# Streamed operands of five matmul stages read in pieces, alternating between the two halves of the tokens

## The chip, the cores and the metric

The kernel runs on one core of one Trainium2 chip. The metric is the device time of one execution in microseconds; lower is better. Two runs of the kernel before gave 889.39 and 889.61 us, a median of 889.5 us.

## The reference, cut to what matters

Two transformer-like blocks are applied in turn to x of shape (1, 256, 1024) in float32: 256 tokens, model width 1024. Nearly all the arithmetic is in dense projections:

```python
xn = rms_norm(h, norm1_g)                       # first block
proj = xn @ w_in                                # 1024 -> 5136
for n, y in enumerate((y_a, y_b, y_c, y_d)):    # four branches, width 512
    merged += sigmoid(xn @ w_gate[n] + b_gate[n]) * (y @ w_branch[n])
h = h + merged @ w_out
h = h + square(relu(rms_norm(h) @ w_ff1)) @ w_ff2          # 1024 -> 4096 -> 1024
h = h + sigmoid(rms_norm(h) @ w_ple_gate + b) * (p @ w_ple)
...                                             # second block, on the result
x = x + g1 * (merged_2 @ w_out_2)
x = x + g2 * ((silu(hh @ w_gate_2) * (hh @ w_up_2)) @ w_down_2)   # 1024 -> 2816 -> 1024
return rms_norm(x, normf_g)
```

Beside the projections there are small parts (spatial gating, gated linear attention, banded attention, a convolution, an mLSTM and a second attention), and a vector of modulations computed from `ada_w_2`.

## The kernel before, in words

Activations are kept transposed, features on the 128 partitions and the 256 tokens along the free dimension (`T = 256`). To keep float32 accuracy with the reduced float32r type of the matrix engine, every operand is split into a high part, rounded to float32r, and a low part, the remainder. Each product is then made of three matmuls: high weights by low tokens (L1054), low weights by high tokens (L1056), high by high (L1057).

Weights arrive from HBM in 298 slabs of 8 units (a unit is a 128x128 block of a weight matrix; `SLAB = 8`), 512 KB each, in the order that `plan()` and `NAMES` give. `sync_program` issues the loads into `raw` (5 buffers), ScalarE's `high_part` (L1991, its instruction is L2002) writes `whi`, and VectorE's `low_part` (L1091, its instruction is L1103) writes `wlo`. Both have 4 buffers (`NHL = 4`), so the two engines can be up to four slabs ahead, and both wait for the matmuls of the slab four before.

`tensor_program` walks over `NAMES`. For a stage of kind "F", which is nearly all of them, the weights are the stationary operand (a weight load of 128 columns ahead of each matmul) and the 256 tokens of one feature block are streamed against them. A PSUM bank of 512 values takes two output blocks of 256 tokens, `half(0)` and `half(1)`; for each pair the loop runs over the K input blocks, and in each over the two output blocks. `bank()` takes three PSUM banks by turns and waits until the pair three before has been drained by ScalarE or VectorE. In stages of kind "T" it is the other way round: the activations are stationary and the weights are streamed, 512 (once 272) columns per matmul (L1025 to L1027). Four stages are `WIDE` and stream 258 tokens.

Between products the queue of TensorE also holds the small parts, as steps at fixed slab numbers (`STEPS`, called through `tick()`). Among these are matmuls in plain float32: transposes of `aacc` (L753), a broadcast in the mLSTM (L790), and single small products that `plain()` issues (L601). VectorE's queue has its own steps at fixed slab numbers; the products with `ada` (L1435) lie between slabs 66 and 149.

The stages that the change touches are "F" stages that aren't `WIDE`: `gt0` to `gt3` (the gates, 64 units each) and `br0` to `br3` (the branches, 32 units each), which run by turns from 131 to 274 us; `ff1` (256 units, 296 to 386 us); `ff2` (256 units, 386 to 476 us, it streams `Fhi` and `Flo`); and `dn` (132 units, 820 to 865 us, it streams `Uhi` and `Ulo`). Three matmuls per unit make 768 for the gates, 384 for the branches, 768 for ff1, 768 for ff2 and 396 for dn: 3084 of the 7171 matmuls that the program states. The stages between and after them, `wo` (from 274 to 296 us), `ple`, `pg`, all `zg` and `zu` (711 to 820 us for those that aren't wide), `dy` and `dz`, are not touched.

In the compiled program's layout every streamed activation block of 256 values (1024 bytes per partition) begins 64 bytes past a multiple of 512 bytes, and every 128-column weight block (512 bytes per partition) begins 128 bytes past one. Two unused tensors, `gap0` and `gap3`, are part of that layout.

Of the kernel before, what the change touches and what calls it, by code (L numbers as in the profile page):

```python
# [179 lines left out]
ROPE = (0, 2, 1, 3)  # L180

LATE = 214

BETWEEN = {40: 3, 68: 7, 183: 5}
STEPS = {
# [87 lines left out]
def build(nc, A, out):  # L273
# [16 lines left out]
    with ctx:  # L290
# [158 lines left out]
        half = lambda j: slice(j * T, (j + 1) * T)  # L449
# [53 lines left out]
        def low(s):  # L503
            return lo_v.at(s)
# [90 lines left out]
        def tensor_program(pe):  # L595
# [3 lines left out]
            def plain(b):  # L599

                pe.matmul(banks[b][:, 0:128], ones[:, :], mats[:, 0:128], start=True, stop=True)  # L601
# [6 lines left out]
            def total(tag, b):  # L608
                w.wait_ge(*ones_v.at("set"))
                w.wait_ge(*added.at(tag, 3))  # L610
                pe.matmul(banks[b][:, 0:T], ones[:, :], acc, start=True, stop=True).then_inc(*summed.up(tag))
# [340 lines left out]
            def bank(name, p):  # L952
                if (name, p) in ASIDE:
                    return banks[ASIDE[name, p]]
                if len(held) >= 3:
                    w.wait_ge(*drained(*held[-3]))
                held.append((name, p))
                return banks[(len(held) - 1) % 3]

            def weights(n=1):  # L960
                nonlocal u
                s, o = u // SLAB, u % SLAB
                if o == 0:
                    w.wait_ge(*hi.at(s))
                    w.wait_ge(*low(s))
                u += n
                at = slice(o * 128, (o + n) * 128)
                return whi[:, s % NHL, at], wlo[:, s % NHL, at]

            def tick():  # L970
                for task in pe_steps.get(u / SLAB - 1, ()):
                    if task in tasks:
                        next(tasks[task], None)
# [34 lines left out]
            for name in NAMES[1:]:  # L1008
                kind, _, _, _, m, K = PLAN[name]
                if name == "ga":  # L1010
                    u += SLAB
                    tick()
                    continue
                if kind == "T":
                    bs = [bank(name, tt) for tt in range(2)]
                    for k in range(K):
                        xh, xl = ready(name, k)
                        wh, wl = weights(PLAN[name][4] // 128)
                        if name == "gk":
                            w.wait_ge(*hi.at(8))  # L1020
                            w.wait_ge(*low(8))
                            wh, wl, m = Ghi[:, k, :], Glo[:, k, :], T + 16
                        for tt in range(2):
                            o, ts, last = bs[tt][:, 0:m], slice(tt * 128, (tt + 1) * 128), k == K - 1
                            pe.matmul(o, xl[:, ts], wh, start=k == 0, stop=False)  # L1025
                            pe.matmul(o, xh[:, ts], wl, start=False, stop=False)  # L1026
                            i = pe.matmul(o, xh[:, ts], wh, start=False, stop=last)  # L1027
                            of = [(name, tt)] * last + [("slab", u // SLAB - 1)] * (tt == 1 and u % SLAB == 0)
                            if (name, tt, last) == ("gv", 1, True):
                                of.append(("slab", u // SLAB))  # L1030
                            if of:
                                i.then_inc(*mm.up(*of))
                        if u % SLAB == 0:
                            tick()
                    continue
                wide = name in WIDE
                for p in range(-(-m // 2)):
                    nt = min(2, m - 2 * p)
                    b = bank(name, p)
                    if wide:  # L1040
                        second = SECOND[name, p]
                        os = [b[:, 0:T + 2], banks[second][:, 0:T + 2]]
                        w.wait_ge(*(red_v.at(5) if name == "mq0" else root.at("r3") if name == "mq1"
                                    else ml_s.at("root", 1, 1)))
                        if name == "zu0":
                            w.wait_ge(*att2_s.at("p", 3, 0))
                    else:
                        os = [b[:, half(j)] for j in range(2)]
                    for k in range(K):
                        xh, xl = ready(name, k)  # L1050
                        for j in range(nt):
                            wh, wl = weights()
                            last = k == K - 1 and j == nt - 1
                            pe.matmul(os[j], wh, xl, start=k == 0 and (wide or j == 0), stop=False,  # L1054
                                      skip_group_check=not wide)
                            pe.matmul(os[j], wl, xh, start=False, stop=False, skip_group_check=not wide)  # L1056
                            i = pe.matmul(os[j], wh, xh, start=False, stop=k == K - 1 if wide else last,  # L1057
                                          skip_group_check=not wide)
                            of = [(name, p)] * last + [("slab", u // SLAB - 1)] * (u % SLAB == 0)
                            if of:  # L1060
                                i.then_inc(*mm.up(*of))
                            if u % (SLAB // 2) == 0 and not last:
                                tick()
                    if (name, p) == ("mq0", 0):
                        w.wait_ge(*aw_v.at(3))
                        w.wait_ge(*aw_v.at("sum"))
                        pe.matmul(banks[6][:, 0:T], ones[:, :], aw2[:, 0:T], start=True, stop=True
                                  ).then_inc(*aw_pe.up("aw"))
                        plain(7)
                    tick()  # L1070
                if name == "ple":
                    total("r3", 3)
                if name == "dz":
                    w.wait_ge(*added.at("r5", 6))
                    for h in range(2):
                        pe.matmul(banks[3 + h][:, 0:1], acc[:, TOK[h]], ones[:, 0:1], start=True, stop=False)
                    for h in range(2):
                        w.wait_ge(*sq.at("r5", 7, h))
                        pe.matmul(banks[3 + h][:, 0:1], t512[1][:, T + 128 * h:T + 128 * h + 128], ones[:, 0:1],
                                  start=False, stop=True).then_inc(*summed.up("r5", h))  # L1080
                    for h in range(2):
                        w.wait_ge(*rstd.at("r5", h))
                        pe.matmul(banks[5 + h][:, 0:128], ones[:, :], t512[0][:, TOK[h]], start=True, stop=True
                                  ).then_inc(*spread_pe.up(h))

        def vector_program(v):
# [4 lines left out]
            def low_part(s):  # L1091
                if s >= NS or s in lows:
                    return
                lows.add(s)
                w.wait_ge(*hi.at(s))
                if s >= NHL:
                    w.wait_ge(*mm.at("slab", s - NHL))
                if s in (8, 9, 10):
                    x, y = narrow(s, raw[:, s % NRAW, :], Ghi)
                    v.tensor_tensor(narrow(s, raw[:, s % NRAW, :], Glo)[1], x, y.bitcast(F32), ALU.subtract  # L1100
                                    ).then_inc(*lo_v.up(s))
                    return
                v.tensor_tensor(wlo[:, s % NHL, :], raw[:, s % NRAW, :], whi[:, s % NHL, :].bitcast(F32),  # L1103
                                ALU.subtract).then_inc(*lo_v.up(s))
# [865 lines left out]
            for name in NAMES:  # L1970
                for what, n in EVENTS[name]:
                    if what == "pair":
# [3 lines left out]
                        continue  # L1976
                    if n == int(n) and n >= 1 and n != LATE:
                        low_part(int(n) + 3)
                    for task in v_steps.get(n, ()):
                        if task in tasks:  # L1980
                            next(tasks[task], None)
                    if n == LATE:
                        low_part(int(n) + 3)
# [534 lines left out]
        def gpsimd_program(g):  # L2518
# [13 lines left out]
            g.memset(mpad[:, :, 0:3], 0.0).then_inc(*mpad_g.up("set"))  # L2532

        programs = ((sync_program, nc.sync), (tensor_program, nc.tensor), (vector_program, nc.vector),
                    (scalar_program, nc.scalar), (gpsimd_program, nc.gpsimd))
        for program, _ in programs:
# [127 lines left out]
```

## Time and profile before

| | |
|---|---|
| runs | 889.39 and 889.61 us, median 889.5 us |
| profiled execution, span | 888.8 us, from the first to the last instruction |
| around the span | 0.7 us between the span and the median of the runs |
| TensorE busy | 878.6 us (99%) |
| VectorE busy | 729.9 us (82%) |
| ScalarE busy | 569.2 us (64%) |
| DMA | 189.83 MB, mean 214 GB/s |
| granted TensorE clock | 0.996 of full speed, mean over the span |

No time of the profiled execution other than its span is recorded, so the span plus 0.7 us stands for it. In the profile a matmul's start is recorded and its end is modelled; matmuls overlap, so a row's duration (276 ns) isn't what a matmul costs. What it costs is the distance between the starts of two that follow each other, called the pitch below. "PEld" is the loading of the stationary operand, which runs beside the matmul before.

### The profile page before, as it was taken

The numbers are of one execution on the slowest core, as the hardware profiler recorded it, in microseconds if no ns is written. First come the engines' busy times: TensorE is split into PE (matmuls) and PEld (weight loads), VectorE is DVE, ScalarE is ACT, GpSimd is POOL, SyncE is SP. The second block draws the span as 40 slices with busy tenths as digits, with TensorE's granted clock in tenths as the row PEclk, the third lists the DMA queues.
The fourth block names the chain that finished last, engine by engine and source line by source line (L and its number), as shares of the span: only waits on it lengthen the run. The fifth ranks groups of instructions, "written<-read, shape, count | busy, mean of one in ns | idle before, by whom it ended". The sixth has DMA issues, their size and how long they took to land.

```text
span 888.8 us, 18455 instructions
## 1 busy us (share of the span) xinstructions
PE 878.6 (99%) x7342; PEld 855.4 (96%) x7342; DVE 729.9 (82%) x1168; ACT 569.2 (64%) x838; POOL 1.9 (0%) x9
## 2 busy tenths in 40 slices
PE   8999999999999999999999999999999999999997
PEld 7999989999999999999999999899999999999996
DVE  6788999899999999898966999988788885555544
ACT  7858467675686777654446868677785664444542
POOL 0000000000000000000000000000000000000000
PEclk9999999999999999999999999999999999999998
DMA  8856446556875789988855576654545566566541
GB/s 313 284 194 224 157 150 207 166 173 229 277 274 189 272 289 347 355 318 324 317 189 170 175 218 197 197 164 127 171 146 173 192 196 195 195 193 197 186 158 48
DMA packets 54550, 189.83 MB, mean 214 GB/s; under 512 B 6193, under 2 KB 8641, under 8 KB 54337
## 3 DMA queue, kind: packets, MB, share of 16 engines
q1 hardware_dynamic: 54320, 188.65, 63.4%
q8 instruction: 59, 0.97, 0.4%
q14 instruction: 27, 0.21, 0.1%
q10 hardware_dynamic: 144, 0.00, 0.0%
HBM read 186.53 MB, written 1.05 MB: 211 GB/s over the span
## 4 chain that ended last, share of the span: by engine, by line
PE 96%; DVE 1%; ACT 1%; DMA 1%; issue 0%; SPq 0%; DVEq 0%; ACTq 0%
PE bank L1054 28%; PE bank L1056 28%; PE bank L1057 28%; PE bank L1025 2%; PE bank L1027 2%; PE bank L1026 2%; DMA H<-in_xT 1%; PE bank L753 1%; PE bank L989 0%; PE bank L996 0%; PE bank L992 0%; ACT whi L2002 0%; DVE wlo L1103 0%; PE bank L855 0%; PE bank L728 0%
## 5 line engine op out<-in xcount | busy, mean ns | idle before, releaser
L2002 ACT ACTIVATE whi<-raw 128x1024 fp32r<-128x1024 f32 x294 | 308.4, 1057 | 191.5 <-PE bank L1057 183.9
L1103 DVE TENSOR_TENSOR wlo<-raw,whi 128x1024 fp32r<-128x1024 f32 x294 | 356.5, 1220 | 86.6 <-ACT whi L2002 85.9
L1054 PE MATMUL bank<-Alo,whi 128*128 128x256 f32 x1336 | 373.5, 280 | 0.0
L1057 PE MATMUL bank<-Ahi,whi 128*128 128x256 f32 x1336 | 369.4, 277 | 0.0
L1056 PE MATMUL bank<-Ahi,wlo 128*128 128x256 f32 x1336 | 369.4, 277 | 0.0
L1054 PEld LDWEIGHTS bank<-Alo,whi 128*128 128x128 f32 x1336 | 250.9, 188 | 2.8 <-issue 2.6
L1056 PEld LDWEIGHTS bank<-Ahi,wlo 128*128 128x128 f32 x1336 | 251.0, 188 | 0.4 <-issue 0.2
L1057 PEld LDWEIGHTS bank<-Ahi,whi 128*128 128x128 f32 x1336 | 250.9, 188 | 0.0
L1056 PE MATMUL bank<-Fhi,wlo 128*128 128x256 f32 (+1 forms) x320 | 88.8, 278 | 0.0
L1057 PE MATMUL bank<-Fhi,whi 128*128 128x256 f32 (+1 forms) x320 | 88.8, 278 | 0.0
L1054 PE MATMUL bank<-Flo,whi 128*128 128x256 f32 x256 | 70.9, 277 | 0.0
L1056 PEld LDWEIGHTS bank<-Fhi,wlo 128*128 128x128 f32 x320 | 60.3, 188 | 0.0
L1057 PEld LDWEIGHTS bank<-Fhi,whi 128*128 128x128 f32 x320 | 60.3, 188 | 0.0
L1435 DVE SCALAR_TENSOR_TENSOR aacc<-araw,shb,aacc 128x1024 f32<-128x1024 f32 x42 | 53.7, 1279 | 1.3 <-DMA araw<-in_ada 1.3
L1054 PE MATMUL bank<-Ylo,whi 128*128 128x256 f32 x192 | 53.6, 279 | 0.0
L1056 PE MATMUL bank<-Yhi,wlo 128*128 128x256 f32 x192 | 53.0, 276 | 0.0
L1057 PE MATMUL bank<-Yhi,whi 128*128 128x256 f32 x192 | 53.0, 276 | 0.0
L1202 DVE SCALAR_TENSOR_TENSOR cv<-ypad,cols,cv 128x256 f32<-128x256 f32 x120 | 51.3, 477 | 0.1
L1057 PE MATMUL bank<-Uhi,whi 128*128 128x256 f32 x176 | 48.6, 276 | 0.0
L1054 PE MATMUL bank<-Ulo,whi 128*128 128x256 f32 x176 | 48.6, 276 | 0.0
L1056 PE MATMUL bank<-Uhi,wlo 128*128 128x256 f32 x176 | 48.6, 276 | 0.0
L1054 PEld LDWEIGHTS bank<-Flo,whi 128*128 128x128 f32 x256 | 48.1, 188 | 0.0
(432 smaller groups left out, 1380.8 us busy)
## 6 DMA issues: line engine op xcount, KB each, us to landing
raw<-in_stream SPq DMA_DIRECT2D x298, 512.0 KB, 4.3
araw<-in_ada SPq DMA_DIRECT2D x48, 512.0 KB, 5.9
TB<-in_TB SPq DMA_DIRECT2D x1, 1536.0 KB, 6.9
a8r<-a SPq DMA_DIRECT2D x16, 64.0 KB, 3.9
out<-H SPq DMA_DIRECT2D x4, 256.0 KB, 2.9
bc<-in_bc SPq DMA_DIRECT2D x1, 896.0 KB, 6.0
H<-in_xT SPq DMA_DIRECT2D x1, 512.0 KB, 7.6
mats<-in_mats SPq DMA_DIRECT2D x1, 449.0 KB, 7.1
```

The costliest lines, as they stand in the source:

```text
L753: i = pe.transpose(banks[6 + j // 4][:, j % 4 * 128:j % 4 * 128 + 128], aacc[cb % 2][:, j * 128:j * 128 + 128], ident)
L1025: pe.matmul(o, xl[:, ts], wh, start=k == 0, stop=False)
L1026: pe.matmul(o, xh[:, ts], wl, start=False, stop=False)
L1027: i = pe.matmul(o, xh[:, ts], wh, start=False, stop=last)
L1054: pe.matmul(os[j], wh, xl, start=k == 0 and (wide or j == 0), stop=False, skip_group_check=not wide)
L1056: pe.matmul(os[j], wl, xh, start=False, stop=False, skip_group_check=not wide)
L1057: i = pe.matmul(os[j], wh, xh, start=False, stop=k == K - 1 if wide else last, skip_group_check=not wide)
L1103: v.tensor_tensor(wlo[:, s % NHL, :], raw[:, s % NRAW, :], whi[:, s % NHL, :].bitcast(F32), ALU.subtract).then_inc(*lo_v.up(s))
L1202: v.scalar_tensor_tensor(out=o, in0=y, scalar=c, in1=o, op0=ALU.mult, op1=ALU.add).then_inc(*conv_v.up("tap", j, ct))
L1435: v.scalar_tensor_tensor(out=o, in0=araw[:, n % 3, :], scalar=csil[:, k:k + 1], in1=o, op0=ALU.mult, op1=ALU.add).then_inc(*ada_v.up(n))
L2002: a.activation(whi[:, s % NHL, :], raw[:, s % NRAW, :], ACT.Copy).then_inc(*hi.up(s))
```

## The change

A table gives a piece length to each of the five stages. The 256 streamed tokens are taken as two halves of 128; the stream takes the first piece of the first half, the first piece of the second half, the second piece of the first half, and so on. The output in PSUM is addressed with the same pattern, so that every result lands where it did before. With the piece length e there are 256/e pieces per matmul, each e values (4e bytes) long. Two pieces that follow each other lie 512 bytes apart, less or more one piece. Nothing else changes: the number and order of instructions, the weight loads, the waits and the transfers stay.

```diff
+PIECES = {"gt": 8, "br": 4, "ff1": 16, "ff2": 32, "dn": 64}
...
+            def in_pieces(name, x):
+
+                e = PIECES.get(name if name in PIECES else name[:2])
+                return x if e is None else x.rearrange("p (h c e) -> p c h e", h=2, e=e)
+
...
                     else:
-                        os = [b[:, half(j)] for j in range(2)]
+                        os = [in_pieces(name, b[:, half(j)]) for j in range(2)]
                     for k in range(K):
-                        xh, xl = ready(name, k)
+                        xh, xl = (in_pieces(name, x) for x in ready(name, k))
```

## Rows read from the trace of the kernel before

**Rows 1.** The page: busy time by engine; the chain that ended last, by engine.
```profile
PE 878.6 (99%) x7342; PEld 855.4 (96%) x7342; DVE 729.9 (82%) x1168; ACT 569.2 (64%) x838; POOL 1.9 (0%) x9
...
PE 96%; DVE 1%; ACT 1%; DMA 1%; issue 0%; SPq 0%; DVEq 0%; ACTq 0%
```

**Rows 2.** Waits: who waited for whom, us in total, times, longest us.
```profile
ACT whi L2002 <- PE bank L1057: 183.9, 132, 3.6
DVE wlo L1103 <- ACT whi L2002: 85.9, 82, 2.7
...
PE bank L989 <- ACT whi L2495: 1.7, 2, 0.9
```

**Rows 3.** Stretches: length, busy us (x instructions) of PE, PEld, DVE, ACT, POOL, clock, DMA.
```profile
191.00:263.00 72.00, 72.00 (x633) 70.71 (x632) 70.92 (x110) 51.02 (x78) 0.00 (x0) 1.00 0.73 250
296.00:386.00 90.00, 90.00 (x795) 89.92 (x794) 85.52 (x103) 66.76 (x93) 0.00 (x0) 1.00 0.92 332
386.00:476.00 90.00, 90.00 (x797) 90.00 (x795) 70.76 (x83) 40.03 (x45) 0.00 (x0) 1.00 0.77 274
722.00:820.00 98.00, 98.00 (x868) 98.00 (x867) 56.89 (x56) 47.38 (x54) 0.00 (x0) 1.00 0.63 201
820.00:865.00 45.00, 45.00 (x400) 45.00 (x399) 23.75 (x25) 22.68 (x26) 0.00 (x0) 1.00 0.55 181
```

**Rows 4.** Timeline of PE in dn and in wo2: start us, duration us, instruction.
```profile
839.83 0.28 PE L1056 MATMUL bank<-Uhi,wlo 128*128 128x256 f32 x1
...
840.96 0.28 PE L1057 MATMUL bank<-Uhi,whi 128*128 128x256 f32 x1
...
679.84 0.28 PE L1054 MATMUL bank<-Mlo,whi 128*128 128x256 f32 x1
...
680.90 0.28 PE L1054 MATMUL bank<-Mlo,whi 128*128 128x256 f32 x1
```

**Rows 5.** Line L1057: duration ns min/median/max, first and last start.
```profile
L1057 PEld LDWEIGHTS bank<-Uhi,whi x176: 187/188/188, 820.1 to 879.6; 128*128 128x128 f32 x176
...
L1057 PEld LDWEIGHTS bank<-Mhi,whi x64: 192/192/192, 676.4 to 698.7; 128*128 128x128 f32 x64
```

**Rows 6.** Timeline of PE after a break at 711 us.
```profile
711.40 0.28 PE L1057 MATMUL bank<-Ahi,whi 128*128 128x256 f32 x1
...
711.76 0.28 PE L1057 MATMUL bank<-Ahi,whi 128*128 128x256 f32 x1
...
711.99 0.28 PE L1056 MATMUL bank<-Ahi,wlo 128*128 128x256 f32 x1
...
712.33 0.28 PE L1056 MATMUL bank<-Ahi,wlo 128*128 128x256 f32 x1
```

**Rows 7.** Timeline of PE: plain float32 matmuls of 256 and of 128 columns.
```profile
565.57 1.02 PE L790 MATMUL bank<-diag,ones 128*128 128x256 f32 x4
...
444.89 1.04 PE L753 MATMUL bank<-mats,aacc 128*128 128x128 f32 x8
```

**Rows 8.** The lines L790 and L753: duration ns min/median/max.
```profile
L790 PE MATMUL bank<-diag,ones x8: 378/379/379, 565.6 to 608.6; 128*128 128x256 f32 x8
...
L753 PE MATMUL bank<-mats,aacc x48: 272/273/328, 259.2 to 445.7; 128*128 128x128 f32 x48
```

**Rows 9.** Timeline of PEld after a break at 510.8 us.
```profile
510.82 0.19 PEld L1054 LDWEIGHTS bank<-Fhi,whi 128*128 128x128 f32 x1 [0.41 <-issue]
510.93 0.19 PEld L1056 LDWEIGHTS bank<-Fhi,wlo 128*128 128x128 f32 x1
```

**Rows 10.** Timeline of PE: float32r matmuls of 512 columns.
```profile
569.89 0.39 PE L1025 MATMUL bank<-whi,Alo 128*128 128x512 f32 x1
...
570.80 0.39 PE L1026 MATMUL bank<-wlo,Ahi 128*128 128x512 f32 x1
```

## The prediction

> **What bounds the kernel now.** I read the page first, for the busy shares and the chain of waits: TensorE is busy for 99% of the span and holds 96% of the chain that ended last [rows 1]. The view of the waits says the same from the other side: ScalarE, which makes the high weights, waits 183.9 us for the matmuls of earlier slabs, VectorE waits 85.9 us behind ScalarE, and the longest entry of TensorE itself is 1.7 us [rows 2]. So the weights are there in time and the time is the number of matmuls times their pitch. The number doesn't change; only the pitch can move.
>
> The pitch comes from the stretches. In the pure product stretch from 820 to 865 us, which is the stage dn, 400 matmuls touch 45.00 us; some three of them only overlap the start, so 397 fill it: 113.4 ns each [rows 3]. The timeline gives the same: ten pitches in 840.96 - 839.83 = 1.13 us, 113 ns [rows 4]. The stretch 722 to 820 has 865 in 98.00 us, again 113.3 ns, though VectorE is busy 58% of it and DMA moves 201 GB/s; the stretch 386 to 476 has it too (794 in 90.00, among them a few smaller ones) at 79% and 274 GB/s [rows 3]. So the pitch doesn't depend on what the other engines and the transfers do to the memory. The granted clock in all these rows is 1.00, the upper level of 2.4 GHz, at which 256 columns are 106.7 ns. Of the 113.3 ns, 6.6 ns aren't columns.
>
> Are they a fixed cost? Three views say no. First, the same instruction with the same operand positions has another pitch elsewhere: in wo2 nine pitches take 680.90 - 679.84 = 1.06 us, 117.8 ns [rows 4], and there the weight loads of L1057 take 192 ns where those of dn take 188 ns [rows 5]. Second, after a break at 711 us three pitches take 711.76 - 711.40 = 0.36 us, and soon after three take 712.33 - 711.99 = 0.34 us, 120 ns and then 113 ns without any change of instruction [rows 6]. Third, plain float32 matmuls, which stream at half the rate, show almost nothing on top of their columns: the four of L790 last 1.02 us together and 0.379 us each, so three pitches are 0.64 us, 214 ns, against 213.3 ns for 2 x 256 columns (the rounding of the row leaves +/- 3 ns); the eight of L753 give (1.04 - 0.273)/7 = 109.6 ns against 106.7 ns for 2 x 128 [rows 7, 8]. 512 columns of float32r take (570.80 - 569.89)/4 = 228 ns against 213.3 ns [rows 10]. What remains over the columns is 1 to 3 ns for a stream at half rate and 6.6, 11 or 14 ns at full rate, in steps of some 4.5 ns (117.8 - 113.3; 192 - 188). I read such a step as one meeting: the stream of tokens and the stream of the next weights read the same partitions at once, and where they come to the same part of the memory one of them stalls.
>
> **The change part by part.** Instructions, their order, waits and transfers stay, so nothing is queued anew behind a waiting instruction. What moves is the order of addresses in 3084 matmuls.
>
> Before: in one pitch the weight stream covers 512 bytes and the token stream 1024. If memory parts repeat every 512 bytes, the token stream overtakes the weights exactly once per matmul wherever the two start. That is the one step that the 113.3 ns hold. A float32 stream at half rate never overtakes. After: the halves lie 512 bytes apart, so both look alike to the rule, and by turns the token stream goes twice over each piece while the weights go once over the same length. Its mean speed is that of the weights; it only swings ahead and back by half a piece, 2e bytes: 8 bytes for br, 16 for gt, 32 for ff1, 64 for ff2, 128 for dn. The starts are 64 bytes apart (64 and 128 past the multiple of 512). Pieces of 4, 8 and 16 then never meet the weights, 32 just reaches, 64 goes past.
>
> The price of the step for a stage: floor 109.2 ns (the 109.6 ns of L753, whose rounding allows 109; 109.2 is 106.7 plus the 2.5 ns that the half-rate rows leave), so 113.3 - 109.2 = 4.1 ns are to be had. The weight loads allow it: the first two after the break at 510.8 us start 0.11 us apart while no matmul holds them [rows 9], which bounds a load's own pitch to 105 to 115 ns. That row is the weak place; if 113 were the loads' own pitch, nothing would be gained (rival B).
>
> - gt, br, ff1, ff2: 768 + 384 + 768 + 768 = 2688 matmuls by 4.1 ns = 11.0 us. Bounds: 0 below; above, 6.6 ns each (the columns alone) = 17.7 us.
> - dn: 396 matmuls. With pieces of 64 the stream still passes the weights. One meeting as before would give 0, none -1.6 us, two +1.6 us. I take 0.
> - The jumps themselves: no row shows a stream or a PSUM write with a jump in it. I take 0, since the nearest rows, all contiguous, show a cost only with meetings. Bounds: nothing, to one step (4.1 ns) for each jump; 256/e - 1 jumps are 31, 63, 15, 7 and 3 per matmul, 66,084 in all, 271 us. A range that wide is carried by rivals D and E.
> - Cover by VectorE: from 191 to 263 us it is busy 70.92 of 72.00 us [rows 3]. Some 576 changed matmuls lie there, so TensorE alone would need 72.0 - 2.4 = 69.6 us, and VectorE becomes late by up to 1.3 us. It can hand most of that on, since it may be four slabs ahead and the stretch after it is looser; ff1 needs 85.52 us of VectorE and would have 90.0 - 3.1 = 86.9 [rows 3], so it holds. I take 0.5 us lost, bounds 0 and 2.
> - After effects: wo, ple, pg, dy and dz start from another relation of the two streams and may fall into the 117.8 ns rhythm of wo2. All of wo at it costs 192 x 4.5 ns = 0.9 us. I take 0.3, bounds 0 and 2.
>
> Sum against the profiled execution: 888.8 + 0.7 - 11.0 + 0.5 + 0.3 = 879.3 us. The span plus 0.7 us is the median of the runs, so the forecast for the runs is 879.3 us too, 1.1% less.
>
> What the trace can't answer is the price of jumps in the output. The Trainium skill's page "PSUM — Partial Sum Buffer", section "Specifications (TRN2)", gives cachelines of 8 bytes and says "any non-contiguous AP slows matmuls significantly"; no run here shows it, since every output of the kernel before is contiguous. By its letter this is rival E; all pieces here hold at least two whole pairs, so by the reason it gives, the changed stages would lose little.
>
> **The rivals.** B, nothing changes: the 113 ns are the pitch of the weight loads or a fixed cost. For it: it is the commonest pitch by far and very even. Against it: rows 4 to 6. It gives 889.5 us, give or take 1.
>
> C, slower by meetings where pieces are long. Place: ff2 and dn. With pieces of 32 and 64 the stream swings past the weights 256/2/e times, 4 and 2 times per matmul, where it passed once before. Price: 3 x 4.1 ns x 768 + 1 x 4.1 x 396 = 9.4 + 1.6 = 11.0 us, against 1920 x 4.1 ns = 7.9 us gained in the other three stages: 889.5 - 7.9 + 11.0 = 892.6 us. It decides from the point where the real distance of the two streams is under 64 bytes; the 64 bytes are those of the start addresses, and when the reads of each begin relative to the other I can't see. With a distance under 32 bytes ff1 turns too (8 meetings, +22 us).
>
> D, each jump costs: an address pattern of three dimensions that loses one cycle of the lower clock level, 0.83 ns (a fifth of the step), at each of 66,084 jumps would add 55 us: 944 us, with gates and branches hit most (+26 and +52 ns per matmul). A third of that still is 908 us. For it: no row shows such a pattern running free. Against it: nothing.
>
> E, writing in pieces halves the pace: 214 ns, the float32 pitch of [rows 7], for 113: 3084 x 0.10 = 310 us, 1200 us.
>
> **How the numbers follow.** The forecast has 0.45, with its own range 876 to 884 us. B 0.17, C 0.21 (885 to 899), D 0.14, E 0.03. The measurement of this kernel can tell about 2% from no change, which is 17.8 us. Faster by more needs 5.8 ns of the 6.6 per matmul gone, or a slower pitch elsewhere cured as well: 0.03, out of the forecast's tail. Slower by more than 2% is most of D, E and the bad end of C: 0.14. Within: 0.83. The range is 875.5 to 903 us: it leaves 0.04 below and about 0.15 above. The likeliest case, C and B together lie within it.
>
> **What would show it.** In the profile after: pitch of 109 ns in gt, br, ff1 and ff2 (the stretch of ff2 holds 825 matmuls in 90 us where it held 794), 113 in dn and in the untouched zg and zu, weight loads at 188 ns throughout, waits of ScalarE for TensorE smaller. C would show as ff2 slower and gt faster; D as a pitch that rises with the number of jumps, br worst; B as 113 everywhere. Wrong would be the idea itself if the pitch falls evenly in all five stages whatever the piece, dn included, or if it rises most where pieces are short.

## The result and the profile after

The changed kernel takes 911.17 us (910.23 and 912.11) against 889.5: the two medians make 1.0244, and the ratio with its interval is 1.0252 (95% interval 1.0236 to 1.0269). It is slower by 21.7 us where 10.2 us less was forecast, and outside the range. Two executions in the runs below had a much lower granted clock (1476.88 us at 0.56 in the kernel before, 1096.78 us at 0.75 in e9) and are left out of every median and ratio. The profiled execution has a span of 910.8 us, 22.0 more than before.

TensorE is as busy as it was, it only does the same number of matmuls at a longer pitch, and ScalarE waits longer for it. First the page and the waits of the kernel after:

```profile
PE 901.1 (99%) x7342; PEld 877.7 (96%) x7342; DVE 732.1 (80%) x1168; ACT 572.7 (63%) x838; POOL 1.9 (0%) x9
...
ACT whi L2009 <- PE bank L1064: 195.7, 136, 3.6
```

PE's busy time rose by 22.5 us, VectorE's by 2.2: the cover by VectorE that the prediction worried about was never used up, because nothing got faster. Now the stretches of the kernel after (length, busy us and instructions of PE, PEld, DVE, ACT, POOL, clock, DMA share and rate): ff1, ff2, pg and dn.

```profile
308.00:402.00 94.00, 94.00 (x786) 93.94 (x785) 85.05 (x102) 67.69 (x92) 0.00 (x0) 1.00 0.90 317
404.00:497.00 93.00, 93.00 (x787) 93.00 (x786) 70.55 (x82) 39.64 (x44) 0.00 (x0) 1.00 0.76 262
503.00:526.00 23.00, 23.00 (x196) 22.95 (x195) 19.34 (x30) 19.07 (x33) 0.00 (x0) 1.00 0.57 181
842.00:887.00 45.00, 45.00 (x400) 45.00 (x399) 23.92 (x26) 22.39 (x26) 0.00 (x0) 1.00 0.58 184
```

ff1 has 786 matmuls in 94 us, so 94.00/783 = 120 ns each, where it had 90.00/792 = 114 [rows 3]. ff2 has 93.00/784 = 119 ns for 90.00/794 = 113. dn has 400 in 45 us, exactly what it had. The timelines of PE give each stage's pitch without the small matmuls in between (start us, duration us). First gates (16 pitches apart), then a branch, ff1 and ff2 (24 pitches apart each):

```profile
139.97 0.28 PE L1061 MATMUL bank<-Alo,whi 128*128 128x256 f32 x1
...
141.94 0.28 PE L1063 MATMUL bank<-Ahi,wlo 128*128 128x256 f32 x1
...
280.50 0.30 PE L1064 MATMUL bank<-Yhi,whi 128*128 128x256 f32 x1
...
283.54 0.29 PE L1064 MATMUL bank<-Yhi,whi 128*128 128x256 f32 x1
...
330.52 0.28 PE L1061 MATMUL bank<-Alo,whi 128*128 128x256 f32 x1
...
333.40 0.28 PE L1061 MATMUL bank<-Alo,whi 128*128 128x256 f32 x1
...
440.52 0.28 PE L1063 MATMUL bank<-Fhi,wlo 128*128 128x256 f32 x1
...
443.37 0.28 PE L1063 MATMUL bank<-Fhi,wlo 128*128 128x256 f32 x1
```

That is 1.97/16 = 123 ns in the gates (pieces of 8), 3.04/24 = 126.7 in the branches (4), 2.88/24 = 120.0 in ff1 (16) and 2.85/24 = 118.8 in ff2 (32), against 113.3 in all of them before. [rows 3] and [rows 4] show that for ff2 and dn; here are gates and a branch of the kernel before, 24 pitches apart, 2.72 us each:

```profile
142.75 0.28 PE L1056 MATMUL bank<-Ahi,wlo 128*128 128x256 f32 x1
...
145.47 0.28 PE L1056 MATMUL bank<-Ahi,wlo 128*128 128x256 f32 x1
...
267.74 0.28 PE L1057 MATMUL bank<-Yhi,whi 128*128 128x256 f32 x1
...
270.46 0.28 PE L1057 MATMUL bank<-Yhi,whi 128*128 128x256 f32 x1
```

By pitches the loss is 768 x 10.0 + 384 x 13.4 + 768 x 6.7 + 768 x 5.5 ns = 7.7 + 5.1 + 5.1 + 4.2 = 22.1 us. By the starts in the traces it is a little less: gt0 starts at 130.59 us before and 130.63 after, ple, the first stage behind ff2, at 475.92 and 497.45. So gates and branches took 12.3 us more, ff1 5.0 and ff2 4.1, 21.5 in all; ple and pg, which aren't changed, added 1.0 to 1.1, and some 0.5 us came back behind them. Together that is the 22.0 us of the spans. The first matmul of ple, before and after:

```profile
475.92 0.28 PE L1054 MATMUL bank<-Blo,whi 128*128 128x256 f32 x1
```

```profile
497.45 0.28 PE L1061 MATMUL bank<-Blo,whi 128*128 128x256 f32 x1
```

dn, with pieces of 64, gives nothing. The shorter the piece the longer the pitch, but not in proportion to the jumps: 7, 15, 31 and 63 jumps cost 5.5, 6.7, 10 and 13.4 ns.

### The profile page after: what moved, and what is told of

The parts are those of the page before. It is cut to its first block, busy times and chain, and to the rows that moved or that the text cites. A ratio compares the mean times of both kernels' runs of the same rounds, so it can differ in the third digit from the quotient of the medians.

```text
span 910.8 us, 18455 instructions
## 1 busy us (share of the span) xinstructions
PE 901.1 (99%) x7342; PEld 877.7 (96%) x7342; DVE 732.1 (80%) x1168; ACT 572.7 (63%) x838; POOL 1.9 (0%) x9
## 4 chain that ended last, share of the span: by engine, by line
PE 91%; ACT 4%; DVE 3%; issue 1%; DMA 1%; SPq 0%; DVEq 0%; ACTq 0%
PE bank L1061 27%; PE bank L1063 27%; PE bank L1064 27%; ACT whi L2009 1%; PE bank L1034 1%; PE bank L1032 1%; PE bank L1033 1%; DMA H<-in_xT 1%; PE bank L755 1%; DVE wlo L1110 1%; PE bank L996 0%; PE bank L1003 0%; PE bank L999 0%; DVE mqk L1538 0%; PE bank L857 0%
## 5 line engine op out<-in xcount | busy, mean ns | idle before, releaser
L1061 PE MATMUL bank<-Alo,whi 128*128 128x256 f32 x1336 | 378.0, 283 | 0.0
L1064 PE MATMUL bank<-Ahi,whi 128*128 128x256 f32 x1336 | 373.8, 280 | 0.0
L1063 PE MATMUL bank<-Ahi,wlo 128*128 128x256 f32 x1336 | 373.8, 280 | 0.0
L1061 PE MATMUL bank<-Ylo,whi 128*128 128x256 f32 x192 | 55.5, 289 | 0.0
L1064 PE MATMUL bank<-Yhi,whi 128*128 128x256 f32 x192 | 55.0, 286 | 0.0
L1063 PE MATMUL bank<-Yhi,wlo 128*128 128x256 f32 x192 | 54.9, 286 | 0.0
```

## The experiments

Most of them use one device: the stages zg2 to zu10 of the kernel before are 18 equal stretches of 48 matmuls with no other matmul in between, all at 113.3 ns [rows 3]. A table gives each its own address pattern, so that one execution measures 18 patterns. Its core, on the kernel before:

```diff
+def pieces(e, d=128, off=0):
+    return off, [[e, 128 // e], [d, 2], [1, e]]
+def onward(e, hop):
+    return 0, [[2 * e, 128 // e], [e + hop, 2], [1, e]]
+def shift(off):
+    return off, [[1, 256]]
...
-                        os = [b[:, half(j)] for j in range(2)]
+                        os = [in_slot(name, "w", b[:, half(j)]) for j in range(2)]
...
+                            xh, xl = (in_slot(name, "r", x) for x in (xh, xl))
...
+                            wh, wl = wh[:, cols_of], wl[:, cols_of]
```

`in_slot` replaces the free dimensions by those of the table, `cols_of` cuts the weight columns. A pitch in the tables below is a mean over 24 pitches in the later part of the stage, from the starts in the timeline. Where single pitches swing (with pieces of 4 they go from 120 to 134 ns), another choice of 24 moves the mean by up to 0.5 ns.

**e1: reading or writing, and the size.**

> The kernel before, with patterns only in the quiet stages zg2 to zu10 (48 matmuls each, one pattern per stage): read and written in pieces of 64, 32, 16, 8, 4 (zg2 to zg4); read only in those sizes, written in one run (zg5 to zg7); written only (zg8 to zg10); zu4, zu7, zu10 as before. In the read-only and write-only stages the tokens land in another place in PSUM, so those products stand for other tokens. Theory R (the order of reads costs): the read-only stages have the pitches of the read-and-write ones, as in the changed kernel 113, 119, 120, 123 and 127 ns, and the write-only ones stay at 113. Theory W (the jumps in PSUM cost): the other way round. Both: they share it.

| pieces of | 64 | 32 | 16 | 8 | 4 |
|---|---|---|---|---|---|
| read and written | 113.3 | 118.8 | 120.0 | 123.3 | 126.8 |
| read only | 113.3 | 118.8 | 120.0 | 123.3 | 126.8 |
| written only | 113.3 | 113.3 | 113.3 | 113.3 | 113.3 |

Timeline of PE of e1, 24 pitches apart: zg7, read in pieces of 4, and zg10, written in pieces of 4:

```profile
780.05 0.29 PE L1107 MATMUL bank<-Ahi,wlo 128*128 128x256 f32 x1
...
783.09 0.30 PE L1107 MATMUL bank<-Ahi,wlo 128*128 128x256 f32 x1
...
813.27 0.28 PE L1107 MATMUL bank<-Ahi,wlo 128*128 128x256 f32 x1
...
815.99 0.28 PE L1107 MATMUL bank<-Ahi,wlo 128*128 128x256 f32 x1
```

3.04 us against 2.72 us. The five pitches of the changed kernel come back in another stage, on other data, so they belong to the pattern and not to gates or ff2. All of it is in the reads. Theory R holds, theory W falls.

**e8 and e9: the same at full size.** The reads alone and the writes alone of the change, each in all five stages:

```diff
-                        os = [in_pieces(name, b[:, half(j)]) for j in range(2)]
+                        os = [b[:, half(j)] for j in range(2)]
```

> The changed kernel with the reads in pieces and the writes in one run, in all five stages with the sizes of the change; the tokens of those stages land in another place in PSUM, so their results stand for other tokens. Theory R: the whole loss of the change stays, 911 us. Theory W: 889.5 us.

911.32 us, ratio to the kernel before 1.025 (1.0233 to 1.0266): the whole loss.

```diff
-                        xh, xl = (in_pieces(name, x) for x in ready(name, k))
+                        xh, xl = ready(name, k)
```

> The changed kernel with the writes in pieces and the reads in one run, in all five stages with the sizes of the change; again the results stand for other tokens. Theory R: 889.5 us within 1 us. Theory W, or the rule that output which isn't contiguous slows a matmul: 911 us or most of the way there.

889.37 us, ratio 1.0002 (0.9992 to 1.0012). A stretch of e8, then one of e9, each 94 us in ff1 and what follows it:

```profile
308.00:402.00 94.00, 94.00 (x786) 93.94 (x785) 85.07 (x102) 67.66 (x92) 0.00 (x0) 1.00 0.89 317
```

```profile
308.00:402.00 94.00, 94.00 (x831) 93.96 (x831) 88.96 (x100) 64.95 (x88) 0.00 (x0) 1.00 0.92 329
```

786 matmuls, as in the changed kernel, against 831. With 128 weight columns, writing PSUM in pieces of 4 to 64 values costs nothing that can be measured here. The sentence of the Trainium skill's page "PSUM — Partial Sum Buffer", section "Specifications (TRN2)", that was rival E's ground doesn't hold for these patterns.

**e7: pieces of 64 everywhere.**

```diff
-PIECES = {"gt": 8, "br": 4, "ff1": 16, "ff2": 32, "dn": 64}
+PIECES = {"gt": 64, "br": 64, "ff1": 64, "ff2": 64, "dn": 64}
```

> The changed kernel with pieces of 64 in all five stages; it computes what the kernel before does. Theory P (order within 256 bytes, which pieces of 64 leave as it was): all five stages at 113.3 ns and the time of the kernel before, within 1 us. Theory J with a cost per jump: 3 jumps per matmul would show as under 1 us per 0.3 ns of pitch.

889.41 us, ratio 1.0003 (0.9993 to 1.0012): as said, with 113.3 ns in gates, branches, ff1 and ff2. (Run beside e7 to e9, the kernel before gave 12 times from 887.9 to 888.5 us and 5 from 889.5 to 889.9; what may part them follows.) But its profiled execution took 894.9 us, and there dn was not at 113. Timeline of PE of e7, in zg4 (24 pitches apart), a stage that this kernel doesn't touch:

```profile
744.46 0.28 PE L1063 MATMUL bank<-Ahi,wlo 128*128 128x256 f32 x1
...
747.29 0.28 PE L1063 MATMUL bank<-Ahi,wlo 128*128 128x256 f32 x1
```

2.83/24 = 117.9 ns, and so from zu1 to dz, 1440 matmuls, 6 us; while pa and wo2, at 117.8 in the kernel before, ran at 113.3. It began inside zg1, right after a single pitch of 135 ns. So the rhythm of [rows 4] at 680 us is not tied to the stage or the pattern: it is a second steady relation that an execution may fall into after a disturbance and then keeps. e9's profiled execution (887.71 us) shows wo2 in the quicker rhythm too, 205 matmuls in the stretch that held 197 in the kernel before (shown under e11):

```profile
676.00:699.00 23.00, 23.00 (x205) 23.00 (x204) 19.89 (x33) 14.01 (x22) 0.00 (x0) 1.00 0.55 178
```

The 288 matmuls of pa and wo2 at 4.5 ns are 1.3 us, about what lies between the two groups of times of the kernel before. That this is what parts them is likely, but only profiled executions show their stages. So a difference of 1 us between two medians of these kernels says little.

**e3 and e6: is it the weight stream?** Both cut the weight columns, from 128 to 64 or 32.

> The kernel before, with fewer weight columns in zg2 to zg10, so that the weight stream is shorter; the other output rows of those stages aren't computed anew. 64 columns with the tokens in one run, then in pieces of 64, 32, 16, 8, 4 (read and written), zu5 to zg8 the same with 32 columns (one run, 32, 16, 8, 4), then 64 columns with pieces of 8 and 4 read only and written only. Theory R as meetings: with 64 columns the extra time falls to about half, with 32 to a quarter, so 109 to 111 ns in one run and under 113 in most pieces. Theory J or W: a length of the weight stream changes nothing, 120 ns and more for pieces of 16 and below. A pitch set by the weight loads themselves would fall to 109 ns or below in every stage.

| pieces of (read and written) | one run | 64 | 32 | 16 | 8 | 4 |
|---|---|---|---|---|---|---|
| 64 weight columns | 113.3 | 113.3 | 120.0 | 120.5 | 123.3 | 129.2 |
| 32 weight columns | 113.3 | | 118.3 | 120.0 | 123.3 | 126.8 |

Timeline of PE of e3, 24 pitches apart, with 32 weight columns: zu5 in one run, zu7 in pieces of 4:

```profile
761.34 0.28 PE L1105 MATMUL bank<-Alo,whi 128*32 128x256 f32 x1
...
764.06 0.28 PE L1105 MATMUL bank<-Alo,whi 128*32 128x256 f32 x1
...
784.22 0.29 PE L1105 MATMUL bank<-Alo,whi 128*32 128x256 f32 x1
...
787.26 0.29 PE L1105 MATMUL bank<-Alo,whi 128*32 128x256 f32 x1
```

2.72 us and 3.04 us, to the last digit what they are with 128 columns. A weight stream a quarter as long changes neither the 6.6 ns over the columns nor the cost of pieces. The theory of the prediction falls here on both counts, and so does a pitch set by the weight loads. Two things don't fit. With 64 columns pieces of 32 and of 4 cost 1 to 3 ns more than with 128 or with 32. And 64 columns with pieces of 8 or of 4 written only, which read in one run, ran at 119.0, where in e1 and e9, with 128 columns, such writes cost nothing. Both stages followed stages read in pieces, so something carried over from those may be it, and so may the writes together with 64 columns; this wasn't tried apart.

> The kernel before, with 32 weight columns in single quiet stages (the other output rows aren't computed anew) and the start of the tokens, of the weights or of both shifted, all read in one run; those products stand for other data. Tokens shifted by 16, 32, 48, 64 values; weights shifted by 16, 32, 48, 64, 96; both by 16, both by 32; at the end tokens alone by 16 and 64 with all 128 weight columns. Theory M (the two streams meet, and the place of the weights counts): shifting the weights moves the pitch as shifting the tokens does, and shifting both alike brings back 113.3 ns. Theory T (only the place of the tokens counts): shifting the weights leaves 113.3 ns, shifting the tokens gives 120, 118, 118.5 and 113 or 118 as with 128 columns, and shifting both gives the pitch of the tokens' shift.

With 32 weight columns every one of the eleven patterns ran at 113.3 ns, tokens or weights or both shifted. With 128 columns tokens shifted by 16 gave 120.0, by 64 113.3. Timeline of PE of e6, 24 pitches apart, tokens shifted by 16 values: zg2 with 32 weight columns, zg9 with 128:

```profile
722.45 0.28 PE L1110 MATMUL bank<-Ahi,wlo 128*32 128x256 f32 x1
...
725.17 0.28 PE L1110 MATMUL bank<-Ahi,wlo 128*32 128x256 f32 x1
...
798.94 0.28 PE L1110 MATMUL bank<-Ahi,wlo 128*128 128x256 f32 x1
...
801.82 0.28 PE L1110 MATMUL bank<-Ahi,wlo 128*128 128x256 f32 x1
```

So with a long weight stream the place of the tokens does cost (2.72 us against 2.88). I read that as the two streams meeting, though shifted weights weren't tried with 128 columns. But it is a cost on top of the 113.3 ns that the layout of the kernel before already avoids, not the one inside them. Neither theory as stated passes: M said that the place of the weights would show at 32 columns, T that the tokens' would.

**e2: shifts with all the weight columns.**

> The kernel before, with the start of the streamed tokens in zg2 to zu10 shifted by 8, 16, 32, 48, 64, 80, 96, 112, 120 values against the weights: in zg the read is in one run, in zu in pieces of 16, both written in one run. The products there stand for shifted tokens. Theory R as meetings of the two streams: the pitch depends on the shift, a run in one between 109 and 118 ns, and in pieces of 16 there are shifts at 109 ns (never meeting) beside shifts above 120 ns. Theory J (a jump costs by itself, wherever the weights are): no dependence on the shift by more than the alignment, 113 in one run and about 120 in pieces. Theory W: all 113.

| shift of the tokens (values) | 8 | 16 | 32 | 48 | 64 | 80 | 96 | 112 | 120 |
|---|---|---|---|---|---|---|---|---|---|
| in one run | 118.3 | 120.0 | 117.8 | 118.5 | 117.8 | 120.0 | 117.8 | 118.5 | 117.3 |
| pieces of 16 | 120.0 | 120.0 | 120.0 | 120.0 | 120.0 | 120.0 | 120.0 | 120.0 | 120.0 |

In one run, shifts that differ by 64 values (16 and 80, 48 and 112, 32 and 96) agree, and 16 and 48 don't: the repeat is 64 values, 256 bytes, not the 512 that the prediction took. No shift comes near 109 ns. 64 gave 117.8 here and 113.3 in e6, the two rhythms of one pattern. The single pitches of 32 and 96 run as those of 64 do (117, 118 and 118 ns by turns), so their 117.8 may be that rhythm and not the shift. In pieces of 16 the place of the weights doesn't matter at all.

**e4: other distances between the two regions.**

> The kernel before, with other distances between the two regions read by turns (read only, written in one run, always from the first four feature blocks, so those products stand for other data): pieces of 16 at distances of 128, 32, 136, 144, 160, 192, 224, 256 and 64 values, pieces of 4 at 128, 144, 160, 192, 256, 512 and 64. Theory R as meetings with a repeat of 512 bytes: 128, 256 and 512 alike, 192 and 64 (half a repeat off) different. Theory J: all distances alike, about 120 ns for 16 and 127 for 4. Theory W: all 113.

| distance (values) | 128 | 32 | 64 | 136 | 144 | 160 | 192 | 224 | 256 | 512 |
|---|---|---|---|---|---|---|---|---|---|---|
| pieces of 16 | 120.0 | 123.3 | 120.0 | 120.0 | 120.0 | 123.3 | 120.0 | 123.3 | 120.0 | |
| pieces of 4 | 126.6 | | 126.5 | | 123.3 | 120.0 | 126.6 | | 126.3 | 126.5 |

Distances that are whole multiples of 64 values are alike, those with half of 64 over (32, 160, 224) differ. That gives the repeat of 256 bytes a second time, now from one operand alone, and theory J, by which every distance is alike, falls.

**e5: jumps that keep the order.**

> The kernel before, with other read patterns in single quiet stages (read only, written in one run, from the first four feature blocks; those products stand for other data). First onward patterns, in which every second piece is taken from a place farther on so that the address within 256 bytes runs on as in one run: pieces of 4 with a hop of 64 and 128 values, of 8, 16 and 32 with a hop of 64. Then the same with hops that break it: pieces of 4 with 32, 16, 8, pieces of 16 with 32 and 16. Then pieces of 64 by turns at distances of 160 and 192, of 32 at 64, of 2 at 128. Theory P (what counts is the order of addresses within 256 bytes): the whole onward patterns stay at 113 ns (or 118, its second rhythm) however many jumps they have, the broken ones and pieces of 64 at 160 lie above, pieces of 64 at 192 stay at 113. Theory J (each jump costs): onward pieces of 4 cost as much as pieces of 4 by turns, 127 ns, and pieces of 2 more, over 130.

| pattern, read only | jumps | pitch |
|---|---|---|
| onward, pieces of 4, hop 64 or 128 | 63 | 113.3 |
| onward, pieces of 8, 16, 32, hop 64 | 31, 15, 7 | 113.3 |
| onward, pieces of 4, hop 16 | 63 | 113.3 |
| onward, pieces of 4, hop 32 or 8 | 63 | 120.0 |
| onward, pieces of 16, hop 32 or 16 | 15 | 117.8 |
| by turns, pieces of 64, distance 192 | 3 | 113.3 |
| by turns, pieces of 64, distance 160 | 3 | 120.0 |
| by turns, pieces of 32, distance 64 | 7 | 118.7 |
| by turns, pieces of 2, distance 128 | 127 | 166.7 |

Timeline of PE of e5, 24 pitches apart: zg2 (onward, pieces of 4, hop 64), zg9 (pieces of 64 at 160), zu9 (pieces of 64 at 192), zu10 (pieces of 2):

```profile
721.49 0.28 PE L1108 MATMUL bank<-Alo,whi 128*128 128x256 f32 x1
...
724.21 0.28 PE L1108 MATMUL bank<-Alo,whi 128*128 128x256 f32 x1
...
798.44 0.28 PE L1108 MATMUL bank<-Alo,whi 128*128 128x256 f32 x1
...
801.32 0.28 PE L1108 MATMUL bank<-Alo,whi 128*128 128x256 f32 x1
...
804.41 0.28 PE L1111 MATMUL bank<-Ahi,whi 128*128 128x256 f32 x1
...
807.13 0.28 PE L1111 MATMUL bank<-Ahi,whi 128*128 128x256 f32 x1
...
815.83 0.34 PE L1110 MATMUL bank<-Ahi,wlo 128*128 128x256 f32 x1
...
819.83 0.34 PE L1110 MATMUL bank<-Ahi,wlo 128*128 128x256 f32 x1
```

This is the pair that decides. 63 jumps that leave the order of addresses within 256 bytes as it was take 2.72 us for 24, the same as none; 3 jumps that break it by 32 values take 2.88. A jump by itself is free; the order within 256 bytes is what is paid for. Pieces of 64 are one whole repeat each, so by turns between halves 512 bytes apart they are, to the memory, the order of before: that is why dn didn't move. (Pieces of 4 with a hop of 16 are free too, which theory P as stated doesn't say: not every other order costs.)

**e10: what the 6.6 ns are, and which costs are the token stream's own.**

> The kernel before, with 32 weight columns in single quiet stages, where e3 and e6 left 113.3 ns (other output rows aren't computed anew, and the products stand for other or fewer tokens). Streams of 64, 128, 192 and 240 values in one run; the same 8 and the same 64 values read over and over; then onward pieces of 4 with hops of 32 and 8, of 16 with 32 and 16, pieces of 64 at a distance of 160, pieces of 2, pieces of 4 at 160; at the end 8 values over and over with 128 weight columns. If the 6.6 ns over the columns are a fixed cost of a matmul: pitches of 33, 60, 87 and 107 ns for the four lengths (n/2.4 + 6.6), unless a load holds them at some floor. If they are lost along the stream: n x 0.4427, so 28, 57, 85 and 106 ns. If only addresses matter, 8 values over and over change the pitch, to 107 or far above 113; if it is a fixed cost, it stays 113.3. For the broken patterns: if their cost came from the weight stream, 32 columns bring them to 113.3; if from the token stream alone, they keep 120, 120, 118, 118, 120, 167, 120.

| stream of (32 weight columns, one run) | 128 | 192 | 240 | 256 (e3) | 8 values, 32 times over |
|---|---|---|---|---|---|
| pitch | 60.0 | 86.7 | 106.7 | 113.3 | 110.0 |
| less n/2.4 | 6.7 | 6.7 | 6.7 | 6.7 | 3.3 |

Timeline of PE of e10: zg3, 128 values, and zg5, the same 8 values over and over, 24 pitches apart:

```profile
728.55 0.22 PE L1116 MATMUL bank<-Alo,whi 128*32 128x128 f32 x1
...
729.99 0.22 PE L1116 MATMUL bank<-Alo,whi 128*32 128x128 f32 x1
...
746.64 0.27 PE L1118 MATMUL bank<-Ahi,wlo 128*32 128x256 f32 x1
...
749.28 0.27 PE L1118 MATMUL bank<-Ahi,wlo 128*32 128x256 f32 x1
```

1.44/24 = 60.0 ns for 128 columns of 53.3. The time over the columns is 6.7 ns at all four lengths: up to 256 columns it is a cost per float32r matmul and not one along the stream. Half of it goes when the addresses never leave 32 bytes, so it isn't wholly fixed, but that stream computes nothing of use (the same 64 values over and over stay at 113.3). Beyond 256 columns it is more: the 258 columns of mq1 in the kernel before take 2.90/24 = 120.8 ns, 13.3 over, and 512 columns 228, 14 over [rows 10]. Whether a longer stream pays twice wasn't tried, nor were other lengths with 128 weight columns.

```profile
518.90 0.28 PE L1054 MATMUL bank<-Fhi,whi 128*128 128x258 f32 x1
...
521.80 0.28 PE L1054 MATMUL bank<-Fhi,whi 128*128 128x258 f32 x1
```

(64 values gave pitches of 28 to 38 ns and decide nothing.) The broken patterns at 32 weight columns: onward pieces of 4 with hops of 32 and 8 fell from 120.0 to 113.3, so their cost in e5 hung on the weight stream; onward pieces of 16 with hops of 32 and 16 stayed at 117.8, pieces of 64 at 160 at 120.0, pieces of 2 at 166.7, pieces of 4 at 160 at 120.0. 8 values over and over took 111.7 ns with 128 weight columns.

**e11: breaking the second rhythm.** Two small float32 products more in the kernel before.

```diff
-BETWEEN = {40: 3, 68: 7, 183: 5}
+BETWEEN = {40: 3, 68: 7, 183: 5, 219: 3, 223: 3}
```

> The kernel before (same results), with one small plain float32 product more at the start of pa and one at the start of wo2, stages that run at 117.8 ns with weight loads of 192 ns. If the slower rhythm is a lasting relation between the token stream and the weight loads, and the break at 711 us ended it by its float32 product, these two put 288 matmuls to 113.3 ns: -1.3 us, +0.4 us for the products, so about 888.6 for 889.5. If the rhythm belongs to the place in the program, nothing changes but +0.4 us.

889.34 us, ratio 1.0002 (0.9993 to 1.0011): no change that these times can show; the 0.9 us less that was the first expectation is as large as the spread between executions. In its trace wo2 did go to 113.3 ns, 205 matmuls in a stretch that held 197, while pa stayed at 117.8. The stretch 676 to 699 us, of the kernel before and then of e11:

```profile
676.00:699.00 23.00, 23.00 (x197) 23.00 (x197) 20.11 (x32) 13.29 (x21) 0.00 (x0) 1.00 0.54 176
```

```profile
676.00:699.00 23.00, 23.00 (x205) 23.00 (x204) 20.15 (x34) 13.96 (x22) 0.00 (x0) 1.00 0.56 179
```

That the product did it isn't shown: wo2 ran at 113.3 ns without any product in seven of the other twelve traces (e3, e4, e5, e7, e8, e9, e10). For it speaks only that in those twelve pa and wo2 always had the same rhythm, and here, with the product between them, they don't. In pa the product changed nothing, so it is no switch.

## Why the prediction was wrong

What bounds the kernel was right: TensorE's pitch, and a longer pitch in 2688 matmuls came through as time nearly in full (21.5 of 22.1 us). Two steps of the sum failed. The first promised a gain that wasn't there; the second put at nothing what turned the sign.

- **The first step that failed, the 11.0 us: "Of the 113.3 ns, 6.6 ns aren't columns. Are they a fixed cost? Three views say no."** For every stream of the tokens in this kernel up to 256 columns they are: 6.7 ns at 128, 192, 240 and 256 values with a weight stream a quarter as long (e10, e3), and no shift brings them down (e6, e2). The gain was 0. The three views were real but spoke of something else. The 117.8 ns of wo2 and its loads of 192 ns, and the 120 ns after the break, are costs on top of the 113.3; I took the step between 113.3 and 117.8 and read it downwards, as if there were another one below. And the float32 rows, which have less than 3 ns over their columns, are another kind of matmul, not the same one without a meeting. The floor of 109.2 ns, built on them, was met by no stream that computes something; 8 values over and over came to 110.0. No stretch of before showed a float32r pitch below 113.3 ns; that should have weighed as rival B's evidence. B itself was half right: right about the 6.6 ns, wrong about the change.
- **The second step that failed, 22 us put at 0: the halves "look alike to the rule", and "The jumps themselves ... I take 0".** The prediction saw that the token stream goes twice over each piece, but priced only meetings with the weights. Except in whole pieces of 256 bytes, taking the halves by turns costs by itself: 118.3, 120.0, 123.3 and 126.8 ns with 32 weight columns, about what it is with 128. So the cost lies in the order of the tokens' own reads. The repeat is 256 bytes (e2, e4, e5) and not the 512 of the prediction; by either the two halves fall on the same parts, so that error alone would not have turned the sign. Jumps by themselves are free where they keep the order, and so are the writes (e5, e9), so D and E had the wrong mechanism. But the term stood for all that the pieces cost, and D had the right sign and the right order of the stages: 63 jumps cost 13.4 ns where D had 52.
- **dn at 0**: right, but not because one meeting stayed as before: pieces of 64 leave the order within 256 bytes as it was.
- **C**, slower by meetings where pieces are long, had the wrong end: ff2 was slower, by 4.2 us where C had 9.4, but the short pieces cost most.
- **Cover by VectorE**, 0.5 us: not called on. **After effects**, 0.3 us: ple and pg fell into the slower rhythm, and the stretch at 503 us holds 196 matmuls in 23 us. The loads of ple tell it: of the kernel after, then of before (duration ns min/median/max):

```profile
L1064 PEld LDWEIGHTS bank<-Bhi,whi x16: 188/192/192, 497.6 to 502.9; 128*128 128x128 f32 x16
```

```profile
L1057 PEld LDWEIGHTS bank<-Bhi,whi x16: 187/188/188, 476.0 to 481.1; 128*128 128x128 f32 x16
```

240 matmuls at 4.5 ns are 1.1 us, more than the 0.3 and less than the bound of 2.

The last sentence of the prediction named what would prove the idea wrong: the pitch rising most where pieces are short. It did. What stays open is which part of the memory is busy with what when two visits to the same part of 256 bytes follow closely: the table of e5 and e10 gives costs for orders, not a mechanism (onward pieces of 4 with a hop of 16 are free, of 16 with 16 are not, and pieces of 16 at 160 are dearer than at 128 while pieces of 4 are cheaper).

## What to carry to other kernels

Before a pitch is split into columns and a remainder that could be won, find one instance of the same instruction without the remainder; if thousands show none, take it for a fixed cost until an experiment with another length says otherwise. Stream the moving operand in one run, or in an order that runs on through each 256 bytes; jumps between such parts, and PSUM outputs in pieces of four values or more (with 128 weight columns), were free here. Choose the start of the streamed blocks against that of the weight blocks by a run: 16 values of shift cost 6.7 ns on 113.

## What the runs showed of the hardware that was not expected

- A float32r matmul of n streamed columns has a pitch of n/2.4 + 6.7 ns for n = 128, 192, 240 and 256 with 32 weight columns, and for 256 with 128 (e10, e3); it is 3.3 ns over n/2.4 when the same 8 values are read throughout. At 258 columns it is 13.3 ns over (before).
- The pitch depends on the order of read addresses within 256 bytes: 113.3 to 126.8 ns for by turns in pieces of 64 to 4, and 166.7 ns in pieces of 2 (e1, e5).
- PSUM written in pieces of 4 to 64 costs nothing with 128 weight columns: ratio to the kernel before 1.0002, at most 1.0012 (e9).
- The page "TensorE: Matmul & The Clock Gate" of the Trainium skill, in its section "Step-by-step: what each phase is for", says that loading the next weights takes no SBUF read bandwidth from the running matmul. With tokens shifted by 16 values that isn't so: 120.0 ns with 128 weight columns, 113.3 with 32 (e6).
- The same instructions have two steady rhythms, 113.3 and 117.8 ns. One execution of e7 kept the slower through more than 1440 matmuls and took 894.9 us where the median is 889.41.
